# First attention's value products of a head pair in the two column halves of TensorE's array, instead of zero-padded full-width products one head at a time

## The reference, cut to what matters

```
for qb in 4 blocks of 128 queries, for each of 8 heads:
    o_cmp = masked_softmax(q @ kc.T) @ vc           # 31 compressed keys
    o_sel = masked_softmax(q @ ks.T) @ vs           # causal, branch b = 0
    o_win = masked_softmax(q @ kw.T) @ vw           # causal, branch b = 1
    o     = g0 * o_cmp + g1 * o_sel + g2 * o_win
mix = concat(o_nsa, o_hgrn); x = x + mix @ w_out; then the feed-forward part
```

## Time and profile before

| | |
|---|---|
| median of 3 runs | 1951.29 us (1951.29 to 1951.83) |
| the profiled execution's own time | 1951.9 us |
| its span in the trace | 1950.1 us |
| granted TensorE clock, mean | 0.997 |
| PE busy | 1896.6 us, 97% of the span |
| DVE busy | 1198.2 us, 61% |
| ACT busy | 777.5 us, 40% |
| the 320 instructions of L1064 (160 products of `vl`) | 168.8 to 342.5 us after the start |

### The profile page before, as it was taken

One profiled execution on the slowest core, in us unless ns is written; L12 is line 12 of the kernel. 1 busy time (PEld: TensorE's weight loads), 2 busy tenths in 40 slices (PEclk: granted clock), 3 DMA queues, 4 the chain that ended last, 5 costly groups with the idle time before them and its releaser, 6 DMA issues.

```text
span 1950.1 us, 24487 instructions
## 1 busy us (share of the span) xinstructions
PE 1896.6 (97%) x9230; PEld 1521.2 (78%) x9230; DVE 1198.2 (61%) x2121; ACT 777.5 (40%) x1708; POOL 268.9 (14%) x212
## 2 busy tenths in 40 slices
PE   6999999999999999999999999999999899999999
PEld 4887777888888888766678888888866688888887
DVE  7467898755454465588765545446889765445453
ACT  4445666332232232466633223223366633223231
POOL 3000342111010011111021101011111011011010
PEclk9999999999999999999999999999999999999999
DMA  5232000233333323322123333332421033333332
GB/s 216 62 97 66 23 1 1 87 96 96 95 96 95 97 86 106 99 75 71 49 87 97 98 97 97 95 97 84 128 74 50 29 96 97 98 98 97 98 92 92
DMA packets 51253, 166.55 MB, mean 85 GB/s; under 512 B 6849, under 2 KB 7233, under 8 KB 50881
## 3 DMA queue, kind: packets, MB, share of 16 engines
q1 hardware_dynamic: 51136, 165.00, 27.6%
HBM read 155.01 MB, written 2.10 MB: 81 GB/s over the span
## 4 chain that ended last, share of the span: by engine, by line
PE 84%; DVE 10%; issue 2%; ACT 1%; DMA 1%; SPq 1%; DVEq 0%; ACTq 0%
PE bank L890 24%; PE bank L892 24%; PE bank L891 24%; PE bank L1000 2%; DVE SM L1660 1%; PE bank L864 1%; PE bank L866 1%; PE bank L865 1%; PE bank L1040 1%; PE bank L913 1%; PE bank L1064 1%; PE bank L1073 1%; DVE HX L1819 1%; DVE WL L1444 1%; PE bank L1002 1%
## 5 line engine op out<-in xcount | busy, mean ns | idle before, releaser
L1169 ACT ACTIVATE WH<-RAW 128x512 fp32r<-128x512 f32 (+2 forms) x584 | 331.1, 613 | 794.2 <-PE bank L892 710.9
L1444 DVE TENSOR_TENSOR WL<-RAW,WH 128x512 fp32r<-128x512 f32 (+2 forms) x584 | 449.4, 803 | 72.8 <-ACT WH L1169 66.4
L890 PE MATMUL bank<-HH,WH 128*128 128x512 f32 x1056 | 425.9, 403 | 19.1 <-DVE WL L1444 9.8
L890 PE MATMUL bank<-GH,WH 128*128 128x512 f32 x1088 | 434.2, 399 | 3.6 <-DVE GL L1717 3.4
L892 PE MATMUL bank<-GH,WL 128*128 128x512 f32 x1088 | 424.0, 390 | 0.0
L891 PE MATMUL bank<-GL,WH 128*128 128x512 f32 x1088 | 423.6, 389 | 0.0
L892 PE MATMUL bank<-HH,WL 128*128 128x512 f32 x1056 | 413.9, 392 | 0.0
L891 PE MATMUL bank<-HL,WH 128*128 128x512 f32 x1056 | 413.4, 392 | 0.0
L890 PEld LDWEIGHTS bank<-HH,WH 128*128 128x128 f32 x1056 | 199.9, 189 | 65.6 <-DVE WL L1444 9.8
L890 PEld LDWEIGHTS bank<-GH,WH 128*128 128x128 f32 x1088 | 204.4, 188 | 48.0 <-DVE GL L1717 4.2
L892 PEld LDWEIGHTS bank<-GH,WL 128*128 128x128 f32 x1088 | 204.2, 188 | 42.9
(11 more groups left out here) (219 smaller groups left out, 1983.3 us busy)
## 6 DMA issues: line engine op xcount, KB each, us to landing
RAW<-in_wgu SPq DMA_DIRECT2D x132, 512.0 KB, 3.5
RAW<-in_wd SPq DMA_DIRECT2D x48, 512.0 KB, 3.5
RAW<-in_wd SPq DMA_DIRECT2D x24, 384.0 KB, 3.1
RAW<-in_da_qk SPq DMA_DIRECT2D x16, 512.0 KB, 3.5
TMP<-TMP SPq DMA_DIRECT2D x104, 64.0 KB, 2.0
RAW<-in_w_inh SPq DMA_DIRECT2D x12, 512.0 KB, 3.6
RAW<-in_w_in SPq DMA_DIRECT2D x8, 512.0 KB, 6.6
RAW<-in_w_out SPq DMA_DIRECT2D x8, 512.0 KB, 3.6
```

The source lines that it names most:

```text
L890: e.matmul(b, w_h, hi[st.x][k], start=(k == 0), stop=False)
L1169: e.activation(whs[s % NW][:, a:b], raw[s % NR][:, a:b], ACT.Copy).then_inc(S["wh"], 1)
L1444: e.tensor_tensor(wls[s % NR][:, a:b], raw[s % NR][:, a:b], whs[s % NW][:, a:b].bitcast(F), ALU.subtract).then_inc(S["wl"], 1)
```

## The change

Both heads of a pair are multiplied in one step, at odd n. For each key block j there are now two products, each of 64 stationary columns (`vp` holds the bare values: 64 columns, no zeros) with 128 moving columns: the even head's output goes to partitions 0:64 of bank 7, the odd head's to 64:128. The transposed weights of both heads must be there, so there are four buffers `pts_n` for this attention (two of them the unused `tmp[4:6]`), and `tc` of n waits for `vl` of the pair before the last one rather than for step n-2. GpSimd writes no zeros for `vp` any more, and `e_vg` doesn't wait for them. The rest of the diff is the plan's own picture of this: a `vl` at odd n alone, with the assumed duration that one head had.

```
             g = base + i
             o.add("PE", ("tn", a, i), w // 128 * 110, ("wt", a, i), ("tc", *chain[g - 1]) if i else prior)
-            o.add("ACT", ("tc", a, i), 100 + w, ("tn", a, i), ("vl", *chain[g - 2]) if g >= 2 else None)
+            if a == "n":
+                used = ("vl", a, i // 2 * 2 - 3) if i >= 4 else None
+            else:
+                used = ("vl", *chain[g - 2]) if g >= 66 else ("vl", "n", 63)
+            o.add("ACT", ("tc", a, i), 100 + w, ("tn", a, i), used)
...
-    o.add("POOL", ("zerosg",), 6000, ("pos_in",), ("pag", 7))
+    o.add("POOL", ("zerosg",), 3000, ("pos_in",), ("pag", 7))
...
-        o.add("PE", ("vl", "n", n), w // 128 * 230 + (900 if n % 16 == 0 else 0), ("tc", "n", n), ("e_vgv", 3),
-              n % 16 == 0 and (("nom", n // 16 - 1) if n else ("c_va", 1)))
+        if n % 2:
+            o.add("PE", ("vl", "n", n), w // 128 * 230 + (900 if n % 16 == 1 else 0), ("tc", "n", n), ("e_vgv", 3),
+                  n % 16 == 1 and (("nom", n // 16 - 1) if n > 1 else ("c_va", 1)))
...
-        VP, PTC = p1(8, 6 * T), p1(14, 2 * T)
+        VP, PTC = p1(10, 2 * T), p1(14, 2 * T)
...
-        pts = pb[4:6]
+        pts_n, pts = pb[4:6] + tmp[4:6], pb[4:6]
...
                     for j in range(i + 1):
-                        v = vp[:, j, 2 * b + h // 4, :]
-                        v = v[:, 64:192] if h % 2 == 0 else v[:, 0:128]
-                        done = e.matmul(ob[:, cols], v, pt[:, j * 128:(j + 1) * 128], start=False,
-                                        stop=(n % 16 == 15 and j == i), skip_group_check=True)
+                        for c in range(2):
+                            done = e.matmul(ob[64 * c:64 * c + 64, cols], vp[:, j, 2 * b + h // 4, :],
+                                            pts_n[(n - 1 + c) % 4][:, j * 128:(j + 1) * 128], start=False,
+                                            stop=(n % 16 == 15 and j == i), skip_group_check=True)
+                            if j == i and c == 0:
+                                done.then_inc(S["vl"], 1)
...
-                if g >= 2:
+                if a == "n":
+                    p.wait_ge(S["vl"], g // 2 * 2 - 2)
+                else:
                     p.wait_ge(S["vl"], g - 1)
...
-                p.wait_ge(S["zeros"], 4)
                 e.tensor_scalar(g, b[:, 256:280], r_, None, ALU.mult).then_inc(S["gt_v"], 1)
-                e.tensor_scalar(vp[:, i, :, 64:128], b[:, 0:256].rearrange("p (b c) -> p b c", b=4), r_, None,
+                e.tensor_scalar(vp[:, i, :, :], b[:, 0:256].rearrange("p (b c) -> p b c", b=4), r_, None,
...
-                e.memset(VP, 0.0).then_inc(S["zeros"], 1)
```

More of the change, by code:

```diff
@@ L385, in plan @@
     for i in range(4):
-        o.add("DVE", ("e_vgv", i), 700, of("vg", i), ("lz5a", 0), ("zerosg",))
+        o.add("DVE", ("e_vgv", i), 700, of("vg", i), ("lz5a", 0))
         o.add("ACT", ("e_vga", i), 220, ("e_vgv", i))
@@ L1048, in vl @@
                     h, b, i = nsa(n)
-                    if n % 16 == 0:
+                    if n % 16 == 1:
                         p.wait_ge(S["c_vc"], 8)
                         p.wait_ge(S["c_pt"], 4)
-                        if n == 0:
+                        if n == 1:
                             p.wait_ge(S["c_kc"], 2)
@@ L1238, in c_ge @@
                 p.wait_ge(S["c_hid"], kv + 1)
-                p.wait_ge(S["zeros"], 4)
+                p.wait_ge(S["zeros"], 3)
                 if kv:
@@ L1312, in tc @@
                 p.wait_ge(S["tp"], g + 1)
-                if g >= 2:
+                if a == "n":
+                    p.wait_ge(S["vl"], g // 2 * 2 - 2)
+                else:
                     p.wait_ge(S["vl"], g - 1)
-                e.activation(pts[g % 2][:, 0:w], ptb[:, 0:w], ACT.Copy).then_inc(S["tc"], 1)
+                pt = pts_n[g % 4] if a == "n" else pts[g % 2]
+                e.activation(pt[:, 0:w], ptb[:, 0:w], ACT.Copy).then_inc(S["tc"], 1)
             def nom(k):
```

## The result

The kernel before took 1951.37 us (median of 6 runs), the changed one **1944.26 us** (6 runs, 1943.15 to 1945.37): a ratio of 0.9964, 95% interval 0.9951 to 0.9976. It is faster, by 7 us, where I had forecast 4.6.

The account below looks back on a forecast made before the run. PE was taken to bound up to 206.9 us and from 337.7 to 344.8, VectorE between 206.9 and 325.1. -2.15 - 1.0 + 0.3 - 1.7 = -4.6 us, set against the median: 1946.7 us, range 1943.5 to 1953.5.

Parts of the forecast that it names:

- (b): 206.9 to 325.1 us, bound by VectorE: work moved out and a vanished wait for scores give -1.0 us.
- (a): Stretch up to `e_hv1` 10 at 206.9 us, bound by PE: six pairs instead of 32 products, -2.15 us.
- the fixed part: In each pair's price on PE: 0.37 us for going into the column halves and back, taken from the scores step.
- no overlap: Rival: products in column halves do not overlap, a pair costs 0.37 + 0.446(i+1) us; 1952.9 us, chance 0.13.
- weights exposed: Rival: weight loads not hidden under products of the same rows, 0.64 us a key block; 1958.7 us, chance 0.07.
- (c): 325.1 to 337.7 us, the last head's chain round PE, ACT and DVE, none of them full: +0.3 us.
- (d): 337.7 to 344.8 us, first `tri` of `wo` to the one needing operand 3: -1.7 us.
- PE is full: Claim about 337.7 to 344.8 us: PE busy 7.09 of 7.10 us, so work removed there shortens it one for one.
- What costs nothing: Claim that removing the values' memset changes no time: zeros done at 25.7 us, first values evacuated at 97.5.
- The four buffers take away no wait: Claim that the added buffers remove no wait that VectorE feels, as it waited for scores and `h3`; no gain counted.
- The switch is free: Rival: going into column halves costs nothing, a pair costs 0.213(i+1) us; -7.5 us, 1943.8 us, chance 0.08.

Follow-up runs that it names:

- g1: Changed kernel's order and four buffers, with the old 128-column zero-padded products, one head after the other, and the values' memset moved later: 1947.27 us, 0.9980.
- e3: Changed kernel with a pair's products queued as all key blocks of the left half, then all of the right, instead of alternating: 1947.72 us, 0.9983.
- e1: Kernel before with only the values' memset moved behind the three small ones and the third unit of weights: 1950.51 us, 0.9994.
- e2: Changed kernel with the values' memset, and the waits for it, put back in the old place: 1946.26 us, 0.9973.
- g2: Changed kernel with GpSimd's cast of 128x1024 and three small memsets also moved behind the third unit of weights: 1943.76 us, 0.9965.
- f4: Changed kernel with two buffers for the transposed weights instead of four, the planner being told so: 1951.97 us, 1.0004.
- f3: Changed kernel (pairs in halves, four buffers, no memset) with its instructions in the order of the kernel before: 1949.65 us, 1.0001.

## Why the prediction was right in part

The direction was right and 1944.26 lies in the range, 0.8 us from its lower end. That the sum came out in the range is in part luck: it left out one gain (the memset) and had one place (b) right in sign by another cause than it gave. By the steps:

- **(a) to `e_hv1` 10: right.** Forecast -2.15, measured -2.25 in both pairs of profiles. By g1, 1.25 of it is the pair that now stands behind `e_hv1` 10 (forecast 6 x 0.223 = 1.34) and 1.0 the halves (forecast 0.8, with 0.37 as the fixed part where it is about 0.3). Weight loads of 64 columns took 137 ns each, 16 of them ended within 0.85 us, and they hid entirely: "no overlap" (1952.9) and "weights exposed" (1958.7) are refuted by the 1.02 us of x16. The overlap needs no distance in rows, and it is full where neighbours are in different column halves (e3). The rule of the Trainium skill ("TensorE: Matmul & The Clock Gate", Part 3) that a weight load overlaps with running matmuls only when its row group differs does not hold in this trace: all four loads of a block have the same rows, and the block takes 0.213 us.
- **(b) VectorE's stretch: mis-sized, for want of a term.** Forecast -1.0, measured -2.6 and -2.3. Idle time went from 2.25 to 1.85 us, about what I had. Counted by instructions, two `lo` left (-1.37), one maximum over 384 columns (0.54) and one scaling over 256 (0.55) came in: -0.3, where I had -0.7 and had overlooked the maximum. The busy time fell by 2.25 us (115.9 to 113.7), so nearly 2 us of it is VectorE's own instructions taking less time, a term that the sum did not have. Two groups of them, before and after (L1855 is L1864 of the change, L1805 is L1814):

```profile
L1855 DVE SCALAR_TENSOR_TENSOR P<-P,LBT,SQB 128x512 f32<-128x512 f32 x2 | 2.7, 1348 | 0.0
L1805 DVE TENSOR_TENSOR HX<-HX 128x256 f32<-128x256 f32 x28 | 12.1, 443 | 0.0
...
L1864 DVE SCALAR_TENSOR_TENSOR P<-P,LBT,SQB 128x512 f32<-128x512 f32 x2 | 1.8, 920 | 0.0
L1814 DVE TENSOR_TENSOR HX<-HX 128x256 f32<-128x256 f32 x28 | 14.3, 521 | 0.0
```

  The first fell and the second rose (the second profiles have 1350, 442, 922 and 526); L1836 fell from 1092 to 926 in one profile and stayed at 1088 in the other. All have operands in SBUF, and GpSimd works 48 us of this stretch; that they differ by what GpSimd does beside them is inferred from e1, e2 and g2, not tested here.
- **(c): right**, +0.5 against +0.3 (+1.0 in the first pair, where the clock fell).
- **(d): right where the clock was full.** Forecast -1.7, measured -1.9 to the lazy sum; -0.8 in the first profile, whose `wo` began at half clock. "PE is full" hid that it waits for 1.10 and 0.67 us just before.
- **"What costs nothing": the step that failed.** I asked when the memset's result is needed (97.5 us) and not what it stands beside. It cost 1.7 us up to the first `tn` (e1, e2), and in one profile 2.0 more by a longer wait and the clock. With it the sum is -2.3, -2.3, +0.5, -1.9 and -1.7, -7.7, against the -7.1 of the medians.
- **"The four buffers take away no wait": wrong as a reason.** VectorE felt none in the trace of before, but a pair holds two buffers, and with two in all, and the order that the planner makes of that, the gain is gone (f4; how much is buffers and how much order, it doesn't show). And I had treated the order as a way of carrying the pairs' gain; it is about half of what is left beside the memset (g1), and the pairs are worth nothing without it (f3).
- **"The switch is free" (1943.8)** is nearest to the time, and wrong: its -4.4 in (a) was -2.3. The time came there by the memset.

What stays open: why VectorE's own instructions take longer in the old order and what it loses behind its stretch (f3), and why the clock falls at 1380 and 1540 in one execution and not in another of the same kernel, and for a longer or shorter time at 960 to 990. Two profiles of each kernel don't tell whether the change makes these falls more or less frequent; they move the time by up to 2 us.

## What to carry to other kernels

An instruction taken off an engine with room is not free if another engine was held by it: for every GpSimd instruction that goes or comes, look at the durations of the VectorE instructions beside it, not only at who waits for its result. Small products in two column halves pay when they alternate, are at least two blocks long (of one block a pair costs 0.37 us from start to start and 0.1 around it, against 0.446), and when the order is made for pairs; measured alone, in the old order, they would have been given up. Before a difference of 2 us in 2000 is explained, profile both kernels twice.

## What the runs showed of the hardware

- A GpSimd memset of 128x3072 (2.82 us) holds a VectorE tensor_scalar for 1.7 to 2.2 us (2.18 and 2.64 against 0.48) and does not touch a scalar_tensor_tensor (0.75). A tensor_scalar beside the GpSimd cast of 128x1024 takes 1.25 us instead of 0.47, and the cast 1.50 instead of 1.05 (g2).
- Two column halves of TensorE, fp32, 128 columns streamed: 0.213 us a block for both together, weights of each new; about 0.3 us for going in and out. Queued one behind the other they still come out 0.3 us shorter than at full width (e3).
- TensorE at 1.2 GHz: behind a wait of 1.69 us (24.6 to 26.2 us, before) and behind waits of 1.10 and 0.67 us (326 to 328.3, after) the granted clock was 0.50 for 2 us and more. In other executions, behind a wait of 1.22 us at the first place and the very same two at the second, it stayed at 1.00. Each of these two falls cost about 1.6 us.
